# Rows of the four moving operands of the dense products padded to 272 floats and begun at multiples of 64 bytes

## Time and profile before

| | |
|---|---|
| median of 3 runs | 2476.42 us (2474.61 to 2482.5) |
| span of the profiled execution | 2476.5 us |
| TensorE (matmul) busy | 2418.0 us, 98% |
| VectorE busy | 1562.3 us, 63% |
| ScalarE busy | 1069.0 us, 43% |
| HBM traffic | 527.5 MB, 213 GB/s over the span |
| granted TensorE clock, mean | 0.993 |

### The profile page before, as it was taken

How to read it: one execution, slowest core, us unless ns; L and a number is a source line. 1 busy time by engine, 2 the same in 40 slices (tenths; PEclk the granted TensorE clock), 3 DMA queues, 4 the chain that set the end, 5 groups by cost and what they waited for, 6 DMA issues and landing times. The chain is left out here.

```text
span 2476.5 us, 51025 instructions
## 1 busy us (share of the span) xinstructions
PE 2418.0 (98%) x20476; PEld 2264.4 (91%) x20476; DVE 1562.3 (63%) x2010; ACT 1069.0 (43%) x1263; POOL 94.0 (4%) x180
## 2 busy tenths in 40 slices
PE   7999999999999999999999999999999999999996
PEld 6778862679999999999999999999999999999996
DVE  6777778665775465465465777758755545555556
ACT  3332320454564354354354445445644543533543
POOL 0000014230000000000000010000000000000000
PEclk9999999999999999999999999999999999999998
DMA  9888649896455555555545464444455554444451
GB/s 394 312 317 307 238 162 299 290 325 261 169 203 213 197 209 198 209 195 186 206 176 181 177 216 161 167 171 171 172 185 183 173 186 173 183 172 185 171 185 69
DMA packets 102829, 516.77 MB, mean 209 GB/s; under 512 B 13072, under 2 KB 29520, under 8 KB 56496
## 3 DMA queue, kind: packets, MB, share of 16 engines
q1 hardware_dynamic: 91728, 467.90, 52.6%
q0 software_dynamic: 10976, 47.11, 5.6%
HBM read 508.57 MB, written 18.95 MB: 213 GB/s over the span
## 5 line engine op out<-in xcount | busy, mean ns | idle before, releaser
L1524 DVE TENSOR_TENSOR wlo<-wraw,whi 128x2048 fp32r<-128x2048 f32 x356 | 815.3, 2291 | 593.3 <-ACT whi L1050 592.9
L1050 ACT ACTIVATE whi<-wraw 128x2048 fp32r<-128x2048 f32 x356 | 682.0, 1916 | 1041.2 <-PE psa L434 1035.6
L432 PE MATMUL psa<-xhi,whi 128*128 128x266 f32 (+1 forms) x3632 | 1048.9, 289 | 19.8 <-DVE wlo L1524 16.6
L433 PE MATMUL psa<-xlo,whi 128*128 128x266 f32 (+1 forms) x3632 | 1040.9, 287 | 0.0
L434 PE MATMUL psa<-xhi,wlo 128*128 128x266 f32 (+1 forms) x3632 | 1039.9, 286 | 0.0
L432 PEld LDWEIGHTS psa<-xhi,whi 128*128 128x128 f32 x3632 | 689.3, 190 | 53.4 <-issue 32.9
L433 PEld LDWEIGHTS psa<-xlo,whi 128*128 128x128 f32 x3632 | 689.9, 190 | 0.2
L434 PEld LDWEIGHTS psa<-xhi,wlo 128*128 128x128 f32 x3632 | 687.4, 189 | 0.0
L434 PE MATMUL psa<-hhi,wlo 128*128 128x264 f32 x2048 | 582.2, 284 | 0.0
L433 PE MATMUL psa<-hlo,whi 128*128 128x264 f32 x2048 | 581.9, 284 | 0.0
L432 PE MATMUL psa<-hhi,whi 128*128 128x264 f32 x2048 | 581.6, 284 | 0.0
(11 more groups left out here) (401 smaller groups left out, 1316.3 us busy)
## 6 DMA issues: line engine op xcount, KB each, us to landing
wraw<-in_w SPq DMA_DIRECT2D x356, 1024.0 KB, 4.8
page<-in_cmp SPq DMA_DIRECT2D x128, 384.0 KB, 4.9
kbuf<-in_selk SPq DMA_DIRECT2D x64, 192.0 KB, 3.9
kbuf<-in_selk POOLq DMA_DIRECT2D x64, 192.0 KB, 3.9
vbuf<-in_selv SPq DMA_DIRECT2D x64, 192.0 KB, 4.2
vbuf<-in_selv POOLq DMA_DIRECT2D x64, 192.0 KB, 4.3
o_win<-in_win POOLq DMA_DIRECT2D x8, 1533.0 KB, 8.1
kbuf<-in_wink SPq DMA_DIRECT2D x8, 768.0 KB, 4.7
```

The source lines that it names most:

```text
L432: mm(out, wh, hi[:, k, 0:w], start=(k == 0), stop=False)
L433: mm(out, wh, lo[:, k, 0:w], start=False, stop=False)
L1050: A(whi[:, p % 2, :], wraw[:, p, :], ACT.Copy).then_inc(s.hi_ready, 1)
L1524: V.tensor_tensor(wlo[:, p % 2, :], wraw[:, p, :], whi[:, p % 2, :].bitcast(F32), ALU.subtract).then_inc(s.lo_ready, 1)
```

## The change

Every row of `xhi`, `xlo`, `hhi` and `hlo` becomes 272 floats (1088 bytes, 17 x 64), of which 264 or 266 are read and written as before. The four tensors begin at multiples of 64 bytes, so that each of their rows does. `region_a` is also rounded up to 64, and `base` is (16512 is a multiple of 64 already). No instruction is added or taken away, no width of a matmul changes, and the two lines that wrote whole rows of `hhi` and `hlo` now name their first 264 floats.

```diff
+ROW = NT + 8
-        base = nc.sbuf_base + (-nc.sbuf_base) % 32
+        base = nc.sbuf_base + (-nc.sbuf_base) % 64
-            def __call__(self, name, shape, dt=F32):
+            def __call__(self, name, shape, dt=F32, line=32):
+                self.next += (-self.next) % line
-        xhi = new("xhi", [128, KT, NT + 2], F32R)
-        xlo = new("xlo", [128, KT, NT + 2], F32R)
+        xhi = new("xhi", [128, KT, ROW], F32R, 64)
+        xlo = new("xlo", [128, KT, ROW], F32R, 64)
-        region_a = new.next
-        hhi = new("hhi", [128, KT, NT], F32R)
-        hlo = new("hlo", [128, KT, NT], F32R)
+        region_a = new.next + (-new.next) % 64
+        hhi = new("hhi", [128, KT, ROW], F32R, 64)
+        hlo = new("hlo", [128, KT, ROW], F32R, 64)
-                    A(hhi[:, bass.ds(4 * g + n, 1), :], stage[:, n:n + 1, :], ACT.Copy).then_inc(s.hh_done, 1)
+                    A(hhi[:, bass.ds(4 * g + n, 1), 0:NT], stage[:, n:n + 1, :], ACT.Copy).then_inc(s.hh_done, 1)
-                    V.tensor_tensor(hlo[:, bass.ds(4 * g + n, 1), :], stage[:, n:n + 1, :],
-                                    hhi[:, bass.ds(4 * g + n, 1), :].bitcast(F32), ALU.subtract).then_inc(s.hid_ready, 1)
+                    V.tensor_tensor(hlo[:, bass.ds(4 * g + n, 1), 0:NT], stage[:, n:n + 1, :],
+                                    hhi[:, bass.ds(4 * g + n, 1), 0:NT].bitcast(F32), ALU.subtract).then_inc(s.hid_ready, 1)
```

## The result

The changed kernel takes 2484.06 us (median of 22 runs, 2476.82 to 2486.99), the one before 2478.05 us beside it (22 runs). The ratio is 1.0021, 95% interval 1.0014 to 1.0028: slower by 5.2 us by that ratio (the two medians lie 6.0 us apart), where 13.4 us less were forecast. It is inside the 0.3% that the prediction called no measurable change, but its interval leaves no doubt of the sign, and 2484 lies above the range.

A forecast was written before the change was run, and what follows sets the result against it. TensorE was taken as the bound: number of dense matmuls times start-to-start distance, plus what attention adds. Gains of 9.1 + 1.9 + 2.4 + 0 = 13.4 us took 2476.4 to 2463.0 us; range 2450 to 2479, the forecast's own 2452 to 2469.

The forecast's parts named there:

- Part 1: 266-wide x rows, 7488 matmuls: distance falls to that of h plus two columns, 122.23 ns, gaining 9.1 us.
- the sorting: Distances within groups 11, 16 and 20 sorted by row start; group 11's cut at multiples of 16 bytes, 121.68 against 123.67 ns.
- Parts 2 and 3: 264-wide x rows, groups 10 to 13 and 53 to 56, then 0 to 9: 1.26 ns less each, gaining 1.9 and 2.4 us.
- part 3: 264-wide x rows in groups 0 to 9, 1872 matmuls: shorter distance let through, gaining 2.4 us.
- Part 4: h rows, multiples of 32 before and of 64 after: taken as no gain, 3.9 us kept for the range.
- the forecast's own upper end: Top of the forecast's own range, 2452 to 2469 us: half the difference and nothing from part 3.
- Parts 5 and 6: Copies into padded rows, and page sums with region_a moved by 800 bytes: both taken as zero.
- The 64-byte rule: Rival, chance 0.11: every row start off a multiple of 64 bytes costs 3.4 ns, giving 2434 us.
- Not the start: Rival, chance 0.27: x and h differ by place in SBUF or other traffic, so nothing moves, 2476 us.
- Equal starts collide: Rival, chance 0.12: moving stream and load of next weights always in step, costing 38 us, giving 2514 us.

The follow-up runs named there:

- x280: Kernel before with x rows of 280 floats, beginning in turn at 0 and 32 past a multiple of 64, h as before: 2477.4 us, ratio 0.9994.
- start32: Changed kernel with every row of the four tensors begun 32 bytes past a multiple of 64: 2481.0 us in one run.
- start8: Changed kernel with every row begun 8 bytes past a multiple of 64, pitch still 272 floats: 2488.1 us in one run.
- pitch268: Changed kernel with rows of 268 floats, beginning in turn 0, 48, 32 and 16 past a multiple of 64: 2478.44 us, ratio 1.0002.
- wstart32: Changed kernel with weights whi and wlo begun 32 bytes past a multiple of 64, rows still at multiples of 64: 2479.8 us in one run.
- after_again: Changed kernel, unaltered, profiled once more: 120.55 or 120.56 and 122.78 ns in h groups, 124.17 in x; no total time given.
- h_only: Changed kernel with xhi and xlo as before, so only hhi and hlo get the padded rows: 2484.5 us, ratio 1.0029.
- w_narrow: Kernel before with 24 columns fewer in each dense matmul, the last 24 columns' products left out: 2329.7 us.
- w268_timed: Changed kernel with 268 columns instead of 266 in the wide x groups, the new ones zeros: 2472.94 us (12 runs), ratio 0.9984.
- x_only: Changed kernel with hhi and hlo as before, so only xhi and xlo get the padded rows: 2484.6 us, ratio 1.0030.

## Why the prediction was wrong

**The distances together**, in ns, with 128 columns of weights, by where rows begin past a multiple of 64 bytes, with the number of 16-byte pieces that a row touches:

| rows begin at | 264 columns | 266 columns | 268 columns |
|---|---|---|---|
| before, x: every multiple of 8 | 122.66 (66 or 67, half each) | 123.44 (67) | |
| before, h; x280: 0 and 32 | 121.40; 121.84 (66) | 123.40 (67) | |
| changed: 0 | 120.56, 121.1, 122.78 (66) | 124.17 (67) | 123.33, 123.7 (67) |
| start32: 32 | 121.67 (66) | 124.17 (67) | |
| start8: 8 | 123.05 to 123.9 (67) | 123.33 (67) | |
| pitch268: 0, 48, 32, 16 | 121.56 (66) | 123.89 (67) | 123.58 (67) |
| wstart32: 0, weights at 32 | 121.67 (66) | 123.33 (67) | 124.44 (67) |

Every distance of 66 pieces is at most 122.8, every one of 67 at least 123.0. The two classes lie close together, and within either there is up to 2.2 ns more, so the table alone would prove little. What bears the rule out are the pairs that hold width and pieces apart: 264 columns cost 1.4 ns more for one piece more (`start32` and `start8`), and in two layouts 268 columns cost less than 266, by 0.3 and 0.4 to 0.8 ns, for the same 67 pieces. In a third, with the weights at 32, they cost 1.1 ns more, which neither pieces nor columns give. A piece is four columns, 1.67 ns at 2.4 GHz, but that size isn't what one measures: from 66 pieces to 67 in rows of one pattern it is 1.6 to 2.5 ns (1.56 in `x280`, 1.66 in `wstart32`, 2.33 in `pitch268`, 2.50 in `start32`). The size of the piece is bounded from both sides: with pieces of 32 bytes h's rows at 16 and 48 in `pitch268` would be dear, and they aren't (121.56), and with pieces of 8 bytes `start8` would have cost 264 columns nothing. With 96 columns of weights the border doesn't hold: 67 pieces take 122.22 or 122.78 ns there, 66 take 121.0 to 121.1. The second effect, what is left within a class, is tied to the weights by `wstart32` and the two kernels of 96 columns, and only in part.

**Part 1 is the step that failed.** It put 266 columns from a good start at "that of h plus two columns, 121.40 + 0.83 = 122.23 ns". By pieces it is h plus one, 123.07, since 266 floats touch 67 pieces from whatever multiple of 8 they begin, and it measured 124.17; there was no start to gain for the 7488 matmuls that carried 9.1 of the 13.4 us. I had taken 123.44 - 122.66 = 0.78 ns for the price of two columns. It was the difference between 67 pieces and a mixture of 66 and 67, 0.83 by the piece. The row that warned was named and set aside: within group 16 the sorting gave 0.27 ns where group 11 gave 2. That width gains nothing from a start at a multiple of 16, because it touches 67 pieces either way. On top of that the new layout made it 0.73 ns dearer.

**Parts 2 and 3 were right in kind for the distance.** 264-wide x rows gain: 0.87 ns in groups 0 to 9, 0.6 and 0.9 in the others; by distance 2.8 us in all against 4.3. By the piece alone it is 0.83 ns. That groups 2 to 7 would let it through, as part 3 assumed, didn't hold. They took 200.77 us in place of 201.24 (200.33 in `after_again`), where 1.4 us less were forecast, and in `h_only`, with x's distances as before, they took 200.32. `w_narrow` shows it at size: its distances there are 9.6 ns shorter, 11.1 us for the six groups, and they took 198.79 us, only 2.5 less, while TensorE's waits for `page` rose. First before, then `w_narrow`, in these groups:
```profile
PE psm L468 <- DVE page L1540: 1.0, 2, 0.6
```
```profile
PE psm L468 <- DVE page L1540: 8.5, 15, 1.7
```
So the page work stands right behind TensorE in this stage, with the DMA share at 0.86 before and in `w_narrow`.

**Part 4, h at nothing, failed too.** It cost 4.0 us: of its two main paces most groups took the slow one. No row at 0 showed that before, because there the rows alternated between 0 and 32.

**A slip in the range.** Half the difference and nothing from part 3 is half of 9.1 + 1.9 us, which gives 2471 us as the forecast's own upper end, not 2469. Nothing in the outcome hangs on it.

**Parts 5 and 6** cost nothing: L1408 and L2163 take 425 and 429 ns where they took 425 and 430, and L470 and L1542, the new lines of the page sums, take 498 and 951 ns against 498 and 953.
```profile
L1542 DVE TENSOR_TENSOR page<-page,pe_rep 128x768 f32<-128x768 f32 x128 | 115.9, 951 | 19.7 <-DMA page<-in_cmp 19.6
L470 PE MATMUL psm<-page,const 128*32 128x384 f32 x512 | 54.6, 498 | 3.2 <-DVE page L1542 1.7 <-ACT psums L1079 1.4
L1408 ACT ACTIVATE hhi<-stage 128x264 f32 x96 | 40.8, 425 | 12.9
L2163 DVE TENSOR_TENSOR hlo<-stage,hhi 128x264 f32 x96 | 38.4, 429 | 23.6 <-ACT hhi L1408 23.6
```
**The rivals.** The 64-byte rule falls: 32 isn't dearer than 0. "Not the start" falls, as `start8` makes h 1.7 ns slower than before. "Equal starts collide" is nearest: it named the moving stream in step with the load of weights. The experiments on the weights and `start32` bear out that h's slow pace needs rows and weights at the same place past a multiple of 64. Its price was too high, +3.0 ns for h and +1.8 for the wide x where +0.65 and +0.73 came, and the argument against it (rows at 0 are cheap today) was drawn from rows mixed with others.

**How well the distances explain the times.** Summed as above from each profile, against the ratio times 2478 us:

| kernel | by distances, us | measured, us |
|---|---|---|
| changed | +6.7 | +5.2 (3.5 to 6.9) |
| h_only | +7.4 | +7.2 (4.7 to 9.7) |
| x280 | -3.0 | -1.5 (-4.0 to +1.2) |
| pitch268 | +0.6 | +0.5 (-1.7 to +2.7) |
| w268_timed | -5.5 | -4.0 (-6.2 to -1.7) |
| x_only | +1.7 | +7.4 (4.5 to 10.4) |

Five agree within their intervals, which are 3 to 5 us wide. `x_only` does not: its distances are as expected, and its time is some 3 us or more above them. Its two MLPs are 4.5 us longer than before, as its distances give, and its profiled run was one of its quicker ones (2481.6 us, where its six runs reach from 2479.4 to 2488.8). What lengthens the others stays open. The MLPs are where the distances are proven: in `h_only`, `x280`, `pitch268` and `w268_timed` they are 7.6, -0.1, 3.8 and -1.4 us longer than before, and their distances give the same to 0.1 us.

**Open as well:** what makes one start give 120.56, 121.11 or 122.78 ns. Shown is that inside the MLPs it is fixed by the program, that the spread goes away with a shorter load, with weights or rows moved by 32 bytes, or with rows that don't share a start, and that the effect of one edit can't be added to that of another. That the two reads get in each other's way is an inference. Open, too, is the greater part of what stands above the columns: 264 columns at 2.4 GHz are 110.0 ns and h takes 121.4, 240 are 100.0 and take 112.1, and no kernel here comes nearer to its columns than 10 ns.

The Trainium skill's "Advanced Engine Details and Errata", section "SBUF Cachelines", names lines of 16 bytes, and that is the size found here. Its rule that two accesses in a line give full performance does not hold for this stream: a row begun 8 bytes in has two floats in its first line and still costs h 1.7 ns (1.4 against the start at 32).

## What to carry to other kernels

Where TensorE is busy throughout and loads 128 columns of weights for each matmul, count the 16-byte pieces that a moving fp32r row touches, width and start together, before padding anything: padding helps only where it lowers that count, and a width that is no multiple of four floats pays for the whole piece anyway. Then measure over a whole group, never from a handful of distances: up to 2 ns more depend on the layout as a whole, weights included, and giving all rows the start that the weights have can settle them on the dear side. A regular difference that one's explanation doesn't give (0.27 ns where 2 were due) is worth more than the mean that it does give.

## What the runs showed of the hardware that was not expected

- Two columns more made matmuls quicker: 268 columns at 123.33 to 123.74 ns against 124.17 for 266 from the same rows, and 123.58 against 123.89 at a pitch of 268 floats.
- Identical loops over identical addresses ran at 120.56 and at 122.78 ns for hundreds of us each, the same in two executions, and changed over where two other matmuls came between (group 44: 122.85 ns up to them, 120.6 after).
- Loading 96 instead of 128 columns of weights took 0.4 to 0.7 ns off a matmul in one layout and up to 1.9 in another, though it is the number of moving columns that sets the pace.
- Moving the weights by 32 bytes took x of 266 columns down by 0.84 ns and put x of 268 columns up by 0.7 to 1.1.
- Rows at 32 with weights at 0 and rows at 0 with weights at 32 gave h the same distance, 121.67 ns in every group of the MLPs; both at 0 gave 120.56, 121.11 or 122.78.
